# A key projection moved in front of a query projection: the memory attention of a two-block transformer

## The chip, the cores and the metric

The kernel runs on one core of a Trainium2 chip. The metric is the device time of one launch in microseconds, taken as the median over several executions. The clock of TensorE is given as the share that the throttle granted: 1.00 is 2.4 GHz and 0.50 is 1.2 GHz, its two levels.

## What is computed

Two transformer blocks of two layers each run one after the other on 256 tokens of width 1024. The change touches the second block. Cut to what matters, each of its layers computes

```python
x = x + rmsnorm(merged @ w_out[l], norm_mix_post[l])
h = rmsnorm(x, norm_mem_pre[l])
mem_n = rmsnorm(mem, norm_memkv[l])
# memory_cross_attention(h, mem_n, ...), 4 heads of 128
q = (h @ w_q).reshape(b, s, MEM_HEADS, MEM_HEAD_DIM)
kv = mem_n @ w_kv
k, v = kv[..., :MEM_WIDTH], kv[..., MEM_WIDTH:]
sc = jnp.einsum("bshd,bmhd->bhsm", q, k) * (MEM_HEAD_DIM ** -0.5)
o = softmax(sc) @ v
x = x + rmsnorm(o @ w_o, norm_mem_post[l])
```

The keys and values come from the memory input alone. The query needs x after the mixing output's norm. All of it is in float32: each product of two matrices is made of three products of rounded halves (high x low, low x high, high x high).

## The kernel before, in words

**Weights.** All weights of a layer are a stream of chunks of 128 x 1536 floats in the order in which the jobs use them. `Stream.add` packs each job's tiles behind the one before. SP copies chunk c into `raw[c % 5]` as soon as the chunk five before it is free. ScalarE rounds it into a high part (`split_hi`, L639), VectorE subtracts for the low part (`split_lo`, L650). For the chunks in the set `of_pool` GpSimd makes the low part (`pool_lo`, L663); in the second block these were chunks 0 and 1. High and low parts have four buffers each (`SPLIT = 4`), so the high part of chunk c waits until chunk c - 4 is free (`split_free`). That signal is given by the first suitable matmul behind the last one that reads the chunk (`free_split`).

**Jobs.** A job is a projection into one bank: 16 tiles of 128 x 128 (8 for mk0a and mk0b) with three matmuls of 256 columns each. The jobs here and the chunks that hold their weights are

| job | what | chunks before | chunks after the change |
|---|---|---|---|
| out3 | last quarter of the mixing output | 47, 48 | 47, 48 |
| mk0a | key head 0 | 48 | 48 |
| mk0b | key head 1 | 49 | 49 |
| mq0 | query heads 0 and 1 | 49, 50 | 51, 52 |
| mk1 | key heads 2 and 3 | 51, 52 | 49, 50 |
| mq1 | query heads 2 and 3 | 52, 53 | 52, 53 |
| mv | values | 53 to 56 | 53 to 56 |

Most jobs go through `products`, which calls `free_split` on the first of the three matmuls of every tile. mq0 is in `first_products`: it makes all 32 products with the high part of x first, in the order of x's rows, and the 16 products with the low part of x behind them. Only the latter call `free_split`:

```python
ins = nc.tensor.matmul(dst, whi[c % SPLIT][0:rows, o:o + width], lo[0:rows, k, :], start=False, stop=(k == KD - 1),
                       skip_group_check=True)
left[c] -= 1
if (n, t, k) == (name, len(pl.jobs[name].tiles) - 1, KD - 1):
    ins.then_inc(*s.mark("filled", name))
else:
    free_split(pl, ins)
```

**Order.** A list, `order_b`, is written out by hand. Every engine walks it and does its part of each step. Around the change it is: the jobs out0 to out3, mk0a, the norm of the mixing output (`norm` and `spread` of p1), mk0b, then the four `front` steps and `squares` of n2, then mq0, `adds` of n2, mk1, `mean` of n2, the first scores, mq1 and so on. In the steps

- `spread p1`, VectorE scales y and adds it to x (`vector_post`, L2424 and L2426);
- `front n2`, ScalarE writes the high part of x with the gains (`x_hi`, L926) and VectorE the low part (`x_lo`, L958), eight rows of tiles each;
- `squares n2`, ScalarE squares x (L952) and then splits high parts up to mq0's last chunk + 2;
- `job`, ScalarE and VectorE split up to the job's last chunk + 2 (mk0a and mk0b, in `own_splits`, split nothing) and ScalarE evacuates the job's bank;
- `mem_keys`, ScalarE evacuates mk0a or mk0b (L2321);
- `adds n2`, GpSimd adds the first half of the squares (`pool_norm`, L870 and L872) and VectorE the rest (`vector_adds`, L889, L891 and L894);
- `mean n2`, TensorE sums over the partitions (`tensor_mean`, L966), ScalarE takes the root and VectorE the reciprocal. The query isn't scaled by it: the scores are, in the exponential.

mk0a and mk0b were already placed around the norm of the mixing output, to give TensorE work while x is not yet there.

Of the kernel before, what the change touches and what calls it, by code (L numbers as in the profile page):

```python
# [225 lines left out]
def second_jobs(stream):  # L226
# [36 lines left out]
    for i in range(4):  # L263
        job(f"out{i}", "w_out_2", "merged", cols(i * T, 2), full)
    for name, source, operand, i in (("mk0a", "w_mkv_2", "mem", 0), ("mk0b", "w_mkv_2", "mem", 1), ("mq0", "w_mq_2", "x2", 0), ("mk1", "w_mkv_2", "mem", 2),
                                   ("mq1", "w_mq_2", "x2", 2)):
        job(name, source, operand, cols(i * P, 1 if name.startswith("mk0") else 2), full)
# [135 lines left out]
def transformer(nc, known, stream_a, jobs_a, stream_b, jobs_b, const_at,  # L403
                x_in, mem_in, pos_in, w_a, w_b, gains_a, gains_b, consts, out):
    ctx = ExitStack()
    with ctx:
# [1403 lines left out]
        for i in range(4):  # L1810
# [3 lines left out]
        order_b += [("job", "out0"), ("mem_split", 0), ("job", "out1"), ("mem_split", 1), ("job", "out2"), ("root_table", "out"),  # L1814
                    ("job", "out3"), ("job", "mk0a"), ("mem_keys", "mk0a"), ("norm", "p1"), ("spread", "p1"), ("job", "mk0b")]
        order_b += [("front", ("n2", i)) for i in range(4)] + [("squares", "n2"), ("mem_keys", "mk0b"), ("job", "mq0"), ("adds", "n2"), ("job", "mk1"), ("mean", "n2"),
                    ("exp_table", 0), ("mem_scores", 0), ("mem_scores", 1), ("mem_weights", 0), ("mem_weights", 1), ("job", "mq1"),
# [17 lines left out]
        PRE = {"n1": "norm_mix_pre_2", "n2": "norm_mem_pre_2", "n3": "norm_ffn_pre_2"}  # L1835
        own_splits = {"mk0a", "mk0b"} | {f"{u}{i}" for i in range(1, KF2 // 2) for u in ("ua", "ub")} - {"ua1"}
        QK_B = [j for i in range(3) for j in (f"q{i}", f"k{i}")]
# [32 lines left out]
        for kind, name in order_b:  # L1870
# [14 lines left out]
            "h": (HH2, HL2, lambda k: ("hidden_lo", k))}, ("ua", "ub", "ma", "mb", "mc"))  # L1885
        plan_b.of_pool = {0, 1}

# [393 lines left out]
        def scalar_b(act, l):  # L2281
# [4 lines left out]
            for kind, name in order_b:  # L2286
# [31 lines left out]
                elif kind == "mem_keys":  # L2318
                    act.wait_ge(*s.at(l, "filled", name))
                    h = "ab".index(name[-1])  # L2320
                    nc.scalar.activation(MK[:, h, :], pl.bank(name)[:, 0:T], ACT.Copy).then_inc(*s.mark("mem_qk", name))  # L2321
                elif kind == "exp_table":
# [7 lines left out]
                elif kind == "job":  # L2330
# [36 lines left out]
                    elif name.startswith("gate"):  # L2367
                        i = int(name[4:])
                        act.wait_ge(*s.at(l, "gate_in", i))
                        nc.scalar.activation(GT[:, 2 * i:2 * i + 2, :], GT[:, 2 * i:2 * i + 2, :], ACT.Tanh, scale=0.5).then_inc(*s.mark("gate", i))  # L2370

                    elif name.startswith("out") or name.startswith("mo") or name.startswith("down"):
                        scalar_y(pl, act, l, name)
                    elif name in ("mk0a", "mk0b"):
                        continue
                    elif name == "mv":
                        act.wait_ge(*s.at(l, "filled", name))
                        nc.scalar.activation(MVB[:, 0, 0:PAIR], ps[:, :], ACT.Copy).then_inc(*s.mark("values_first", name))
                    elif name.startswith("mk") or name.startswith("mq"):
                        i = int(name[2])  # L2380
                        act.wait_ge(*s.at(l, "filled", name))
                        dst, sc = (MK, 1.0) if name[1] == "k" else (MQ, MEM_D ** -0.5)
                        nc.scalar.activation(dst[:, 2 * i:2 * i + 2, :], two(ps[:, :]), ACT.Copy, scale=sc).then_inc(*s.mark("mem_qk", name))
                elif kind == "chunks":
# [410 lines left out]
```

## Time and profile before

| | |
|---|---|
| runs | 1670.61, 1670.56 and 1667.18 us, median 1670.56 |
| the profiled execution | 1670.88 us, its span 1669.1 us |
| TensorE busy | 1629.8 us (98% of the span) |
| VectorE busy | 1209.8 us (72%) |
| ScalarE busy | 899.5 us (54%) |
| GpSimd busy | 116.3 us (7%) |
| granted clock, mean | 0.994 |

Matmuls overlap in the records: one is shown with 0.28 us and the next starts about 0.12 us behind it. So a busy TensorE is one whose matmuls follow each other without a hole; how fast they follow is seen from their start times. The stretch around the change is at 929 to 949 us in the first layer of the second block and at 1411 to 1430 us in its second layer. In the trace's names PE is TensorE, DVE is VectorE, ACT is ScalarE, POOL is GpSimd.

### The profile page before, as it was taken

The page shows a single profiled execution, that of the slowest core. Times are in us where ns is not written, and L with a number is a line of the kernel's source. Part 1 is how long each engine was busy: PE and PEld are TensorE (multiplying, and loading weights), DVE is VectorE, ACT ScalarE, POOL GpSimd, SP SyncE. Part 2 cuts the span into 40 slices and gives each one's busy share as a digit, 9 for nine tenths or more (in the row PEclk, how much of TensorE's full clock was granted, in tenths as well). Part 3 has the DMA queues.
Part 4 walks back from the last instruction along what each step waited for, and adds up shares of the span by engine and source line. Part 5 has one row for each costly group of instructions (what it writes and reads, how often), then busy time and mean ns, then how long its engine had stood idle before and what let it go on. Part 6 is the DMA issues. An engine that isn't in the chain of part 4 may idle for free.

```text
span 1669.1 us, 31856 instructions
## 1 busy us (share of the span) xinstructions
PE 1629.8 (98%) x13566; PEld 1578.4 (95%) x13566; DVE 1209.8 (72%) x1785; ACT 899.5 (54%) x1378; POOL 116.3 (7%) x72
## 2 busy tenths in 40 slices
PE   9988999999999999999999999999999999999997
PEld 9977999999879999999999989999999999899997
DVE  5887777647976776487858768984777767679963
ACT  5585644454775444544544665554545546655542
POOL 2020000020110000210000110001100001010000
PEclk9999999999999999999999999999999999999999
DMA  8313556553225655565345535655464454446560
GB/s 294 107 65 106 198 191 200 179 193 129 95 60 190 217 190 188 193 213 198 112 152 176 167 118 173 217 174 176 149 221 163 141 161 166 152 137 205 184 208 33
DMA packets 53598, 275.03 MB, mean 165 GB/s; under 512 B 6480, under 2 KB 7376, under 8 KB 53328
## 3 DMA queue, kind: packets, MB, share of 16 engines
q1 hardware_dynamic: 53312, 271.94, 48.1%
q8 instruction: 107, 1.75, 0.4%
q10 hardware_dynamic: 144, 1.05, 0.2%
q14 instruction: 35, 0.29, 0.1%
HBM read 271.13 MB, written 1.05 MB: 163 GB/s over the span
## 4 chain that ended last, share of the span: by engine, by line
PE 81%; DVE 13%; ACT 3%; issue 2%; DMA 0%; SPq 0%; ACTq 0%; DVEq 0%
PE bank L809 17%; PE bank L811 17%; PE bank L812 17%; PE scores L809 3%; PE scores L811 3%; PE scores L812 3%; DVE weights_lo L650 3%; DVE x_lo L958 2%; PE heads L809 2%; PE heads L811 2%; PE heads L812 2%; ACT probs L1229 1%; PE heads L1967 1%; PE scores L818 1%; DVE x L2426 1%
## 5 line engine op out<-in xcount | busy, mean ns | idle before, releaser
L650 DVE TENSOR_TENSOR weights_lo<-raw,weights_hi 128x1536 fp32r<-128x1536 f32 (+2 forms) x344 | 583.0, 1712 | 221.6 <-ACT weights_hi L639 220.9
L639 ACT ACTIVATE weights_hi<-raw 128x1536 fp32r<-128x1536 f32 (+5 forms) x352 | 500.2, 1440 | 173.0 <-PE bank L812 74.5
L809 PE MATMUL bank<-x_hi,weights_lo 128*128 128x256 f32 (+1 forms) x1556 | 433.8, 279 | 0.3 <-DVE weights_lo L650 0.3
L811 PE MATMUL bank<-x_lo,weights_hi 128*128 128x256 f32 (+1 forms) x1556 | 430.9, 277 | 0.0
L812 PE MATMUL bank<-x_hi,weights_hi 128*128 128x256 f32 (+1 forms) x1556 | 430.8, 277 | 0.0
L809 PEld LDWEIGHTS bank<-x_hi,weights_lo 128*128 128x128 f32 (+1 forms) x1556 | 290.6, 187 | 3.5 <-issue 2.7
L811 PEld LDWEIGHTS bank<-x_lo,weights_hi 128*128 128x128 f32 (+1 forms) x1556 | 290.8, 187 | 0.1
L812 PEld LDWEIGHTS bank<-x_hi,weights_hi 128*128 128x128 f32 (+1 forms) x1556 | 290.8, 187 | 0.0
L809 PE MATMUL bank<-hidden_hi,weights_lo 128*128 128x256 f32 x692 | 191.5, 277 | 2.0 <-DVE hidden_lo L2278 2.0
L811 PE MATMUL bank<-hidden_lo,weights_hi 128*128 128x256 f32 x692 | 191.0, 276 | 0.0
L812 PE MATMUL bank<-hidden_hi,weights_hi 128*128 128x256 f32 x692 | 191.0, 276 | 0.0
L809 PEld LDWEIGHTS bank<-hidden_hi,weights_lo 128*128 128x128 f32 x692 | 129.9, 188 | 2.6 <-DVE hidden_lo L2278 2.4
L811 PEld LDWEIGHTS bank<-hidden_lo,weights_hi 128*128 128x128 f32 x692 | 129.9, 188 | 0.0
L812 PEld LDWEIGHTS bank<-hidden_hi,weights_hi 128*128 128x128 f32 x692 | 129.9, 188 | 0.0
L870 POOL TENSOR_TENSOR squares<-squares 128x512 f32<-128x512 f32 x28 | 48.9, 1745 | 969.6 <-ACT squares L2207 799.3
L809 PE MATMUL scores<-x_hi,weights_lo 128*128 128x256 f32 x400 | 110.4, 276 | 0.0
L811 PE MATMUL scores<-x_lo,weights_hi 128*128 128x256 f32 x400 | 110.4, 276 | 0.0
L812 PE MATMUL scores<-x_hi,weights_hi 128*128 128x256 f32 x400 | 110.4, 276 | 0.0
L809 PEld LDWEIGHTS scores<-x_hi,weights_lo 128*128 128x128 f32 x400 | 75.1, 188 | 0.0
L811 PEld LDWEIGHTS scores<-x_lo,weights_hi 128*128 128x128 f32 x400 | 75.1, 188 | 0.0
L812 PEld LDWEIGHTS scores<-x_hi,weights_hi 128*128 128x128 f32 x400 | 75.1, 188 | 0.0
L809 PE MATMUL heads<-x_hi,weights_lo 128*128 128x256 f32 x256 | 71.1, 278 | 0.4 <-DVE weights_lo L650 0.4
(427 smaller groups left out, 3487.3 us busy)
## 6 DMA issues: line engine op xcount, KB each, us to landing
raw<-in_w_b SPq DMA_DIRECT2D x202, 768.0 KB, 4.3
raw<-in_w_a SPq DMA_DIRECT2D x120, 768.0 KB, 4.3
raw<-in_w_a SPq DMA_DIRECT2D x16, 512.0 KB, 3.6
raw<-in_w_a SPq DMA_DIRECT2D x2, 736.0 KB, 8.4
raw<-in_w_a SPq DMA_DIRECT2D x2, 672.0 KB, 6.9
x<-in_x SPq DMA_DIRECT2D x2, 512.0 KB, 5.2
mem<-in_mem ACTq DMA_DIRECT2D x1, 1024.0 KB, 8.3
raw<-in_w_b SPq DMA_DIRECT2D x2, 512.0 KB, 5.4
```

Source lines behind the costliest of these rows:

```text
L639: nc.scalar.activation(whi[c % SPLIT][:, 0:n], raw[c % RAW][:, 0:n], ACT.Copy).then_inc(*s.mark("weights_hi", c))
L650: nc.vector.tensor_tensor(wlo[c % SPLIT][:, 0:n], raw[c % RAW][:, 0:n], whi[c % SPLIT][:, 0:n].bitcast(F32), ALU.subtract).then_inc(*s.mar ...
L809: ins = nc.tensor.matmul(dst, wl, xh, start=start, stop=False, skip_group_check=skip)
L811: nc.tensor.matmul(dst, wh, xl, start=False, stop=False, skip_group_check=skip)
L812: ins = nc.tensor.matmul(dst, wh, xh, start=False, stop=stop, skip_group_check=skip)
L818: ins = nc.tensor.matmul(dst, xl, wh, start=first, stop=False, skip_group_check=True)
L870: nc.gpsimd.tensor_tensor(sq[:, 0:2, :], sq[:, 0:2, :], sq[:, 2 * n:2 * n + 2, :], ALU.add).then_inc(*s.mark("sq_pairs", (tag, n)))
L958: nc.vector.scalar_tensor_tensor(out=XL[:, k, :], in0=X[:, k, :], scalar=gains(k), in1=XH[:, k, :].bitcast(F32), op0=ALU.mult, op1=ALU.sub ...
L1229: ins = nc.scalar.activation(PA[c][:, m, :], score_bank[c][:, m * T:(m + 1) * T], ACT.Exp, scale=f[:, m:m + 1], bias=ROW[:, r + m:r + m + ...
L1967: ins = nc.tensor.matmul(out_bank[rows, m * P:(m + 1) * P], VB[:, kt, f * DHD:(f + 1) * DHD], PTB[:, g * kts + kt, :], start=(n == 0), sto ...
L2426: nc.vector.tensor_tensor(x, x, y, ALU.add).then_inc(*s.mark("x_new", (tag, last)))
```

## The change

The job mk1 is packed and run in front of mq0, directly behind mk0b. Its evacuation becomes a `mem_keys` step behind the squares, and it is put into `own_splits`, so that it splits nothing ahead. The low part of the chunk behind mk1's last (51) goes to GpSimd.

```diff
-    for name, source, operand, i in (("mk0a", "w_mkv_2", "mem", 0), ("mk0b", "w_mkv_2", "mem", 1), ("mq0", "w_mq_2", "x2", 0), ("mk1", "w_mkv_2", "mem", 2),
+    for name, source, operand, i in (("mk0a", "w_mkv_2", "mem", 0), ("mk0b", "w_mkv_2", "mem", 1), ("mk1", "w_mkv_2", "mem", 2), ("mq0", "w_mq_2", "x2", 0),
                                    ("mq1", "w_mq_2", "x2", 2)):
...
-                    ("job", "out3"), ("job", "mk0a"), ("mem_keys", "mk0a"), ("norm", "p1"), ("spread", "p1"), ("job", "mk0b")]
-        order_b += [("front", ("n2", i)) for i in range(4)] + [("squares", "n2"), ("mem_keys", "mk0b"), ("job", "mq0"), ("adds", "n2"), ("job", "mk1"), ("mean", "n2"),
+                    ("job", "out3"), ("job", "mk0a"), ("mem_keys", "mk0a"), ("norm", "p1"), ("spread", "p1"), ("job", "mk0b"), ("job", "mk1")]
+        order_b += [("front", ("n2", i)) for i in range(4)] + [("squares", "n2"), ("mem_keys", "mk0b"), ("mem_keys", "mk1"), ("job", "mq0"), ("adds", "n2"), ("mean", "n2"),
...
-        own_splits = {"mk0a", "mk0b"} | {f"{u}{i}" for i in range(1, KF2 // 2) for u in ("ua", "ub")} - {"ua1"}
+        own_splits = {"mk0a", "mk0b", "mk1"} | {f"{u}{i}" for i in range(1, KF2 // 2) for u in ("ua", "ub")} - {"ua1"}
...
-        plan_b.of_pool = {0, 1}
+        plan_b.of_pool = {0, 1, plan_b.last_chunk("mk1") + 1}
...
                 elif kind == "mem_keys":
                     act.wait_ge(*s.at(l, "filled", name))
-                    h = "ab".index(name[-1])
-                    nc.scalar.activation(MK[:, h, :], pl.bank(name)[:, 0:T], ACT.Copy).then_inc(*s.mark("mem_qk", name))
+                    if name == "mk1":
+                        nc.scalar.activation(MK[:, 2:4, :], two(pl.bank(name)[:, :]), ACT.Copy).then_inc(*s.mark("mem_qk", name))
+                    else:
+                        h = "ab".index(name[-1])
+                        nc.scalar.activation(MK[:, h, :], pl.bank(name)[:, 0:T], ACT.Copy).then_inc(*s.mark("mem_qk", name))
```

ScalarE's order behind the fronts of n2, first as it was. In these listings a tile's number is that of its place in memory, not the chunk's: `weights_hi_57<-raw_50` is chunk 51, `weights_hi_54<-raw_51` is 52, `weights_hi_55<-raw_52` is 53 and `weights_hi_56<-raw_53` is 54.

```order
L952 ACTIVATE squares<-x 128x512 x4
L639 ACTIVATE weights_hi_57<-raw_50 128x1536 [waits split_free,arrived1]
L639 ACTIVATE weights_hi_54<-raw_51 128x1536 [waits split_free,arrived2]
L2321 ACTIVATE mem_k<-bank 128x256 [waits filled]
L2383 ACTIVATE mem_q<-bank 128x512 [waits filled]
L639 ACTIVATE weights_hi_55<-raw_52 128x1536 [waits split_free,arrived3]
L639 ACTIVATE weights_hi_56<-raw_53 128x1536 [waits split_free,arrived4]
L2383 ACTIVATE mem_k<-bank 128x512 [waits filled]
L972 ACTIVATE norm_root<-turned,row 128x4 [waits norm_mean]
```

The same place with the change.

```order
L952 ACTIVATE squares<-x 128x512 x4
L639 ACTIVATE weights_hi_57<-raw_50 128x1536 [waits split_free,arrived1]
L639 ACTIVATE weights_hi_54<-raw_51 128x1536 [waits split_free,arrived2]
L639 ACTIVATE weights_hi_55<-raw_52 128x1536 [waits split_free,arrived3]
L639 ACTIVATE weights_hi_56<-raw_53 128x1536 [waits split_free,arrived4]
L2324 ACTIVATE mem_k<-bank 128x256 [waits filled]
L2321 ACTIVATE mem_k<-bank 128x512 [waits filled]
L2385 ACTIVATE mem_q<-bank 128x512 [waits filled]
L972 ACTIVATE norm_root<-turned,row 128x4 [waits norm_mean]
```

The high parts of 53 and 54 moved in front of the evacuations of mk0b, mk1 and mq0; those of 51 and 52 stayed where they were.

VectorE's order at the same place, first as it was, from the low parts of x to the reciprocal for the mean. The low parts are those of chunks 51, 52, 53 and 54.

```order
L958 SCALAR_TENSOR_TENSOR x_lo<-x,gains_b,x_hi 128x256 [waits norm_hi] x8
L650 TENSOR_TENSOR weights_lo_61<-raw_50,weights_hi_57 128x1536 [waits weights_hi]
L650 TENSOR_TENSOR weights_lo_58<-raw_51,weights_hi_54 128x1536 [waits weights_hi]
L889 TENSOR_TENSOR squares<-squares 128x512 [waits norm_sq]
L891 TENSOR_TENSOR squares<-squares 128x256 [waits sq_last_pairs]
L894 TENSOR_TENSOR squares<-squares 128x256 [waits sq_first,sq_last]
L650 TENSOR_TENSOR weights_lo_59<-raw_52,weights_hi_55 128x1536 [waits weights_hi]
L650 TENSOR_TENSOR weights_lo_60<-raw_53,weights_hi_56 128x1536 [waits weights_hi]
L977 RECIPROCAL token_factor<-norm_root 128x4 [waits norm_root]
```

The same place with the change.

```order
L958 SCALAR_TENSOR_TENSOR x_lo<-x,gains_b,x_hi 128x256 [waits norm_hi] x8
L650 TENSOR_TENSOR weights_lo_58<-raw_51,weights_hi_54 128x1536 [waits weights_hi]
L650 TENSOR_TENSOR weights_lo_59<-raw_52,weights_hi_55 128x1536 [waits weights_hi]
L650 TENSOR_TENSOR weights_lo_60<-raw_53,weights_hi_56 128x1536 [waits weights_hi]
L889 TENSOR_TENSOR squares<-squares 128x512 [waits norm_sq]
L891 TENSOR_TENSOR squares<-squares 128x256 [waits sq_last_pairs]
L894 TENSOR_TENSOR squares<-squares 128x256 [waits sq_first,sq_last]
L977 RECIPROCAL token_factor<-norm_root 128x4 [waits norm_root]
```

The low part of 51 is gone, and the three sums for n2 moved behind the low parts of 53 and 54.

GpSimd's order with the change, from the sums of p1 to those of n2.

```order
L870 TENSOR_TENSOR squares<-squares 128x512 [waits y_sq]
L870 TENSOR_TENSOR squares<-squares 128x512 [waits sq_pairs,y_sq]
L872 TENSOR_TENSOR squares<-squares 128x256 [waits sq_pairs]
L663 TENSOR_TENSOR weights_lo_61<-raw_50,weights_hi_57 128x1536 [waits weights_hi]
L870 TENSOR_TENSOR squares<-squares 128x512 [waits norm_sq]
L872 TENSOR_TENSOR squares<-squares 128x256 [waits sq_pairs]
```

The fourth row, the low part of 51, is new; the others stood in this order before.

## Rows read from the trace of the kernel before

**Rows 1.** The page: busy time (share of the span), and the chain that ended last.

```profile
PE 1629.8 (98%) x13566; PEld 1578.4 (95%) x13566; DVE 1209.8 (72%) x1785; ACT 899.5 (54%) x1378; POOL 116.3 (7%) x72
...
PE 81%; DVE 13%; ACT 3%; issue 2%; DMA 0%; SPq 0%; ACTq 0%; DVEq 0%
```

**Rows 2.** TensorE's waits, 900 to 980 us: waited for, us in total, times, longest.

```profile
PE bank L762 <- DVE x_lo L958: 1.5, 2, 1.0
```

**Rows 3.** mq0's start to mk1's end, both layers: length, busy us (instructions) by engine, PEclk, DMA.

```profile
932.20:948.60 16.40, 14.47 (x98) 13.14 (x98) 15.80 (x20) 11.17 (x16) 2.17 (x2) 0.90 0.35 110
1414.00:1430.00 16.00, 14.22 (x99) 13.04 (x98) 15.86 (x20) 11.18 (x16) 2.17 (x2) 0.89 0.34 104
```

**Rows 4.** TensorE's timeline, first layer: start, duration, instruction; mk0b, mq0, mk1, mk1, mean.

```profile
929.36 0.36 PE L809 MATMUL bank<-mem_hi,weights_lo 128*128 128x256 f32 x1
...
932.27 0.28 PE L751 MATMUL bank<-x_hi,weights_lo 128*128 128x256 f32 x1
...
941.76 0.55 PE L809 MATMUL bank<-mem_hi,weights_lo 128*128 128x256 f32 x1 [0.15 <-DVE weights_lo L650]
...
947.10 0.28 PE L812 MATMUL bank<-mem_hi,weights_hi 128*128 128x256 f32 x1
...
948.63 0.50 PE L966 MATMUL turned<-const,squares 128*128 128x2 f32 x4
```

**Rows 5.** The chain of waits in order of time, 939 to 942 us.

```profile
939.95 1.68 DVE weights_lo L650
941.63 0.14 issue
941.76 0.55 PE bank L809
```

**Rows 6.** Stretches behind and with idle time, columns as in rows 3.

```profile
941.80:944.30 2.50, 2.50 (x12) 2.50 (x13) 2.46 (x3) 2.50 (x3) 0.00 (x0) 0.51 0.65 179
...
141.50:144.70 3.20, 0.38 (x5) 0.04 (x1) 3.10 (x6) 0.00 (x0) 0.00 (x0) 1.00 0.01 3
144.70:148.80 4.10, 4.10 (x23) 4.10 (x24) 3.46 (x7) 1.70 (x7) 0.00 (x0) 0.60 0.67 177
1186.30:1189.50 3.20, 2.59 (x24) 2.39 (x22) 3.20 (x4) 2.31 (x3) 2.95 (x3) 1.00 0.00 0
```

**Rows 7.** ScalarE's timeline, first layer.

```profile
935.32 0.91 ACT L926 ACTIVATE x_hi<-x,gains_b 128x256 fp32r<-128x256 f32 x2 [0.41 <-DVE x L2426]
...
938.22 2.85 ACT L639 ACTIVATE weights_hi<-raw 128x1536 fp32r<-128x1536 f32 x2
...
941.64 0.60 ACT L2383 ACTIVATE mem_q<-bank 128x512 f32<-128x512 f32 x1 [0.32 <-PE bank L762]
```

**Rows 8.** VectorE's timeline, first layer.

```profile
935.20 4.74 DVE L958 SCALAR_TENSOR_TENSOR x_lo<-x,gains_b,x_hi 128x256 fp32r<-128x256 f32 x8
...
943.21 0.68 DVE L889 TENSOR_TENSOR squares<-squares 128x512 f32<-128x512 f32 x1
...
944.38 0.42 DVE L894 TENSOR_TENSOR squares<-squares 128x256 f32<-128x256 f32 x1
```

**Rows 9.** Groups by shape (busy us, mean ns); single POOL sums; one DVE line's range.

```profile
L663 POOL TENSOR_TENSOR weights_lo<-raw,weights_hi 128x1536 fp32r<-128x1536 f32 x4 | 14.0, 3510 | 175.1 <-ACT weights_hi L639 175.1
...
L650 DVE TENSOR_TENSOR weights_lo<-raw,weights_hi 128x1536 fp32r<-128x1536 f32 x318 | 556.1, 1763 | 217.5 <-ACT weights_hi L639 216.8
...
917.22 2.62 POOL L870 TENSOR_TENSOR squares<-squares 128x512 f32<-128x512 f32 x1 [185.19 <-ACT squares L2207]
...
937.41 1.38 POOL L870 TENSOR_TENSOR squares<-squares 128x512 f32<-128x512 f32 x1 [12.47 <-ACT squares L952]
...
L2077 DVE SCALAR_TENSOR_TENSOR mem_lo<-mem,gains_b,mem_hi x16: 473/480/1524, 912.7 to 1402.1; 128x256 fp32r<-128x256 f32 x16
```

**Rows 10.** DMA issues: median us from issue to landing.

```profile
raw<-in_w_b SPq DMA_DIRECT2D x202, 768.0 KB, 4.3
```

**Rows 11.** Second layer: ScalarE's high parts of 51 and 52, TensorE's mean.

```profile
1420.13 2.84 ACT L639 ACTIVATE weights_hi<-raw 128x1536 fp32r<-128x1536 f32 x2
...
1430.08 0.50 PE L966 MATMUL turned<-const,squares 128*128 128x2 f32 x4
```

More of the change, by code:

```diff
@@ L2373, in scalar_b @@
                         scalar_y(pl, act, l, name)
-                    elif name in ("mk0a", "mk0b"):
+                    elif name in ("mk0a", "mk0b", "mk1"):
                         continue
@@ L2381, in scalar_b @@
                         act.wait_ge(*s.at(l, "filled", name))
-                        dst, sc = (MK, 1.0) if name[1] == "k" else (MQ, MEM_D ** -0.5)
-                        nc.scalar.activation(dst[:, 2 * i:2 * i + 2, :], two(ps[:, :]), ACT.Copy, scale=sc).then_inc(*s.mark("mem_qk", name))
+                        nc.scalar.activation(MQ[:, 2 * i:2 * i + 2, :], two(ps[:, :]), ACT.Copy, scale=MEM_D ** -0.5).then_inc(*s.mark("mem_qk", name))
                 elif kind == "chunks":
```

## The prediction, made before the changed kernel ran

> **What bounds the kernel now.** The page comes first: TensorE is busy for 1629.8 of 1669.1 us, and 81% of the chain that ended last is its own, with 13% VectorE's [rows 1]. So a change helps or harms only where TensorE waits, or runs at the lower of its two clock levels. The table of waits around the memory attention (900 to 980 us) names one stall that this change can touch: `x_lo` from VectorE [rows 2]. The stretches from the start of mq0 to the end of mk1 give its full price: 16.4 us in the first layer and 16.0 in the second, for 96 matmuls [rows 3]. At the full clock a matmul of these jobs follows the one before by 0.117 us (13 steps from 947.10 to 948.63 [rows 4]), so 96 need 11.2 us. About 5 us a layer are lost.
>
> The matmul timeline shows how [rows 4]. mk0b's 24 matmuls start at 929.36 and mq0 follows at 932.27. Its products with `x_lo` are held up twice, by 1.0 us at most [rows 2]. mk1 then starts at 941.76, and the chain there does not run through `x_lo` alone: it goes from `x_lo` to the low part of a chunk (939.95 to 941.63) and from there to mk1's first matmul [rows 5]. That is chunk 51, the first that was not split ahead of the norm. Behind the idle time the granted clock is 0.51 for 2.5 us in which 12 matmuls start, one per 0.21 us [rows 6]. The product for the mean starts at 948.63, and I use it as the finishing line of each layer: behind it both programs have the same order.
>
> **What the change does to it, on TensorE first.** The sum is of where that finishing line moves. mk0b and mk1 need chunks 49 and 50, which are split before the norm, and the mem operand, which is complete long before. So mk1 runs at once: 932.27 + 48 x 0.117 = 937.9. By then all of `x_hi` is written (the eight copies end at 936.2 [rows 7]) and `x_lo` nearly (939.9 [rows 8]). The waits on x are gone. This is the announced gain, and if mq0 could run at 937.9 it would be had in full.
>
> It can't. mq0 now sits in chunks 51 and 52, and ScalarE's place for the high part of chunk 51 has not moved: behind the eight `x_hi` and the four squares, at 938.22 [rows 7]. Two high parts take 2.85 us there, so the first is ready at 939.7. Its low part is now GpSimd's. The four 128x1536 subtractions it did elsewhere took 3.51 us each, against 1.76 for one on VectorE [rows 9]. 939.7 + 3.5 = 943.2, and with the 0.14 us from low part to matmul [rows 5] mq0 starts at 943.35. TensorE has then idled 5.4 us in one piece. `x_lo` is complete, so mq0 runs through: 32 products with `x_hi` are 3.75 us. VectorE has the low part of chunk 52 by 941.1 + 1.75 = 942.9 or, if GpSimd holds it off, by 945.0. The first matmul that needs it is the 19th of mq0, no earlier than 945.4. Cost: nothing.
>
> **The clock.** After a stretch of 3.2 us with hardly a matmul (141.5 to 144.7) the granted clock over the following 4.1 us is 0.60, and after this stage's broken idle time it is 0.51. A stretch of 3.2 us with 24 matmuls in it (1186.3) keeps 1.00 [rows 6]. The idle time of 5.4 us is nearest the first. A clock of 0.60 over 4.1 us loses 0.40 x 4.1 = 1.6 us of matmuls. I take 1.6 us for this idle piece. The Trainium skill (TensorE: Matmul & The Clock Gate, section on HAM oscillation) says that long enough idle time throttles the array again, and that the penalty is half of the throttled time. With that rule every idle piece below costs such an amount; were it not to hold here, the sum would be 6.4 us smaller. The 33rd matmul of mq0, the first with `x_lo`, is then at 943.35 + 3.75 + 1.6 = 948.7.
>
> **A second wait that the diff hardly shows.** ScalarE splits ahead to the chunk two behind mq0's last. That was 52 and is 54 now. The buffers of high and low parts are four, so chunk 54 needs the place of 50, and this is given free only by mk1's successor. mq0 is written by `first_products`, which calls `free_split` on its products with `x_lo` and not on those with `x_hi`. So the high part of 54 starts behind 948.7. Queued behind it on ScalarE are the evacuations of mk0b, mk1 and mq0. On VectorE the low part of 54 is ahead of the three sums for n2, which the mean waits for; before, the sums were in front of the low parts of 53 and 54 [rows 8]. The run from matmul to mean: 0.4 (matmul and signal), 1.5 (high), 1.8 (low), 1.6 (three sums, 943.21 to 944.80 [rows 8]), 0.1: 5.4 us. mq0's own last matmul is 1.9 behind the 33rd, so TensorE idles 3.5 us more, with a second low stretch behind it, 1.6 us. GpSimd's two sums for n2 now stand behind its low part. They end by 945.5, or near 949 if VectorE gets in between, and the sum is wanted at 952. Nothing. Root, table load and exponentials stand behind the mean as before, beside mq1. The three evacuations (0.4, 0.6 and 0.6 us, as mq0's [rows 7]) follow the high part of 54 and end by 952.3, before the scores want them. SP's transfers of chunks 56 and 59 wait for the low parts of 51 and 54 and so start some 1.6 and 4 us later. A chunk lands in 4.3 us [rows 10], so 56 is there at 947.6, and mv, the first job that needs it, is behind mq1. I cost them at nothing. The other copies and evacuations are the same ones in another order.
>
> **The sum.** First layer: the mean at 948.7 + 5.4 = 954.1 in place of 948.63 gives +5.5, and the low stretch behind it +1.6: +7.1. Second layer, from its own rows [rows 11]: high part of 51 from 1420.13 to 1421.6, low to 1425.1, mq0 at 1425.25, 33rd matmul at 1430.6, mean at 1436.0 against 1430.08: +5.9, and +1.6. Together +14.6. No later stage gives it back: what follows is a chain led by TensorE with the same waits. The profiled execution took 1670.88 us (span 1669.1), 0.3 above the median of 1670.56, so I forecast 1685.5 in the profile's terms and 1685.2 against the median.
>
> **Bounds of what isn't shown.** Clock: from nothing in all four pieces (-6.4) to twice the loss behind the long idle (+3.2). GpSimd's part at this place: its 3.51 us were measured where VectorE did nothing. Where VectorE subtracts beside it, a 128x512 sum took 2.62 in place of 1.38 [rows 9], so a VectorE subtraction that gets in first adds up to 1.76 a layer. Below 3.5 nothing speaks for. I take 3.5, since chunk 52's high part comes 1.4 us after chunk 51's, and GpSimd is well under way by then.
>
> **The rivals.** *A, the filler does its work* (faster). The 5 us a layer come back: 1670.6 - 5.1 - 4.8 = 1660.7. The point that decides is whether the low part of 51 is there at 937.9. For it speaks that every operand of mk1 is early and that `x_lo` stalls vanish. Against it stands the order: the high part is behind the squares at 938.2, so even an instant GpSimd leaves TensorE idle to 939.8. 3%. *B, one wait only*: the place of chunk 50 is freed in time or the second chain hides beside mq0. Then the mean is at 943.35 + 5.6 + 1.6 = 950.55, +1.9, and +2.4 in the second layer: 1674.9. 6%. *C, GpSimd is held up by VectorE*: as the forecast with up to 1.76 us more a layer, 1688.7. The Trainium skill (SBUF — State Buffer, on the two separate sides) has the port pair of the two engines as an exclusive lock for a whole instruction. The rows agree in kind: one `mem_lo` took 1.52 us in place of 0.48 with GpSimd at work [rows 9]. In this kernel it costs TensorE something if an `x_lo` or chunk 52 slips in front of chunk 51. 10%. *D, no change*: the new waits happen to equal the old 5 us a layer, 1670.6. 2%. *Forecast*: both waits, with one to two low stretches a layer, 79%.
>
> **How the numbers follow.** A measurement here tells 0.2% (3.3 us) from nothing. Only A gives faster: 0.03, and 0.04 with what I have not thought of. D and a lucky B give the same: 0.02. The rest is slower: 0.94. The range takes in the forecast without any clock loss (1678.8), goes halfway from there to B (1676.5), and up past C to 1690 for more clock loss on top. It leaves out A, D and most of B, 11 in 100, and some of the tails.
>
> **What would show it.** Right: a matmul gap of 5 to 6 us after mk1 near 938 and 1420, released by GpSimd's low part; no wait for `x_lo`; a second gap of 3 to 4 us before the product for the mean, released by VectorE's sums, with the low part of 54 just before them; granted clock under 1 behind both. Wrong on the first step: GpSimd's 128x1536 starts before 938. Wrong on the second: the high part of 54 starts before the products with `x_lo`.

## The result, and the profile after

The changed kernel takes 1687.78 us (median of 4 runs, 1685.58 to 1689.75), the kernel before, run beside it, 1669.08 us (median of 4, 1667.18 to 1670.61). The ratio is 1.0111, with a 95% interval of 1.0098 to 1.0124: slower by 18.7 us. The forecast was 1685.2 us with a range of 1676.5 to 1690, and 94 in 100 for slower. The profiled execution took 1689.03 us (span 1687.2).

The page first, busy time and the chain that ended last, against [rows 1]:

```profile
PE 1633.1 (97%) x13566; PEld 1582.5 (94%) x13566; DVE 1210.5 (72%) x1783; ACT 899.3 (53%) x1378; POOL 128.5 (8%) x74
...
PE 81%; DVE 12%; ACT 3%; issue 2%; POOL 0%; DMA 0%; ACTq 0%; DVEq 0%
```

TensorE has the same number of instructions. It is busy 3.3 us longer, and the span is 18.1 us longer, so most of the difference is time in which TensorE waits. GpSimd has two more instructions and 12.2 us more: two low parts of 3.44 us (6.9), and four sums that together take 5.5 us longer, as shown below. The page's shares say no more than that. The waits of TensorE around the memory attention do, with the columns of [rows 2]:

```profile
PE bank L751 <- issue: 5.5, 1, 5.5
PE turned L966 <- DVE squares L894: 3.3, 1, 3.3
```

The wait for `x_lo` is gone, and two others stand in its place. TensorE's timeline places them; the second of these lines answers to [rows 4] (what was mk1's wait there is mq0's here), and the last three are of the second layer:

```profile
939.93 0.28 PE L812 MATMUL bank<-mem_hi,weights_hi 128*128 128x256 f32 x1
945.73 0.55 PE L751 MATMUL bank<-x_hi,weights_lo 128*128 128x256 f32 x1 [5.53 <-issue]
...
951.10 1.98 PE L762 MATMUL bank<-x_lo,weights_hi 128*128 128x256 f32 x16
956.33 1.02 PE L966 MATMUL turned<-const,squares 128*128 128x2 f32 x4 [3.25 <-DVE squares L894]
...
1434.79 0.55 PE L751 MATMUL bank<-x_hi,weights_lo 128*128 128x256 f32 x1 [5.52 <-issue]
...
1441.31 1.98 PE L762 MATMUL bank<-x_lo,weights_hi 128*128 128x256 f32 x16
1446.54 0.61 PE L966 MATMUL turned<-const,squares 128*128 128x2 f32 x4 [3.25 <-DVE squares L894]
```

The first wait is put down to "issue", that is to nothing that the trace shows. GpSimd's line suggests whom it waits for, and the first experiment below confirms it: the low part of chunk 51 ends at 942.19 + 3.44 = 945.63, and mq0 starts 0.10 us later.

```profile
942.19 3.44 POOL L663 TENSOR_TENSOR weights_lo<-raw,weights_hi 128x1536 fp32r<-128x1536 f32 x1 [14.83 <-ACT weights_hi L639]
945.59 2.79 POOL L870 TENSOR_TENSOR squares<-squares 128x512 f32<-128x512 f32 x1
948.46 2.13 POOL L872 TENSOR_TENSOR squares<-squares 128x256 f32<-128x256 f32 x1
```

The second wait is spelled out by the chain of waits in order of time, from mq0's first product with `x_lo` to the mean: the high part of chunk 54, its low part, and three sums.

```profile
951.26 0.13 PE bank L762
951.43 0.04 issue
951.47 1.50 ACT weights_hi L639
953.00 1.76 DVE weights_lo L650
954.75 0.61 DVE squares L889
955.37 0.02 issue
955.39 0.43 DVE squares L891
955.85 0.43 DVE squares L894
```

VectorE's line in the same stretch, against [rows 8], has two more things to read:

```profile
937.63 3.25 DVE L958 SCALAR_TENSOR_TENSOR x_lo<-x,gains_b,x_hi 128x256 fp32r<-128x256 f32 x8
943.52 6.48 DVE L650 TENSOR_TENSOR weights_lo<-raw,weights_hi 128x1536 fp32r<-128x1536 f32 x2 [2.64 <-ACT weights_hi L639]
953.00 1.76 DVE L650 TENSOR_TENSOR weights_lo<-raw,weights_hi 128x1536 fp32r<-128x1536 f32 x1 [3.00 <-ACT weights_hi L639]
```

The eight `x_lo` take 3.25 us where they took 4.74: GpSimd's sums no longer run beside them. The low parts of chunks 52 and 53 take 6.48 us together where two take 3.4: GpSimd's work runs beside these now.

To compare the kernels I use one ruler throughout: the time from mk0b's first matmul of a layer to the first matmul of mq0, its first product with `x_lo`, the mean, mq1's first matmul, and the first matmul of mv, the values' job behind mq1. Both programs have the same order behind mq1. In us, first layer / second layer:

| | mq0 | x_lo | mean | mq1 | mv |
|---|---|---|---|---|---|
| before | 2.91 / 2.82 | 7.54 / 7.55 | 19.27 / 18.81 | 21.25 / 20.79 | 29.41 / 29.15 |
| changed | 13.95 / 13.93 | 19.32 / 20.45 | 24.55 / 25.68 | 28.62 / 28.80 | 37.97 / 37.59 |
| growth | | | +5.28 / +6.87 | +7.37 / +8.01 | +8.56 / +8.44 |

At mq1's start the change has cost 7.37 + 8.01 = 15.4 us, but TensorE's clock is still low there (the rows follow below), and at mv it has cost 8.56 + 8.44 = 17.0 us. The medians are 18.7 us apart, so 1.7 us of the result are not attributed.

The two profiled executions differ by 18.15. They also differ outside the stage: mk0b's first matmul stands at 931.78 in place of 929.36, 2.4 us later, ahead of the change. A stretch near 41 us, in code that is the same in both, ran at the lower clock in this execution. The columns are those of [rows 3], first the changed kernel, then the one before:

```profile
41.00:45.00 4.00, 4.00 (x22) 4.00 (x21) 0.66 (x4) 1.58 (x2) 0.00 (x0) 0.54 0.41 166
```

```profile
41.00:45.00 4.00, 4.00 (x36) 4.00 (x36) 2.04 (x4) 1.59 (x2) 0.00 (x0) 1.00 0.28 112
```

This does not go with the order of jobs. Of the runs below, both with the old order show it too (0.50 and 0.57 in this stretch), and four with the new order have 1.00 there.

The clock in the stage itself (columns as in [rows 3]; in turn the first wait, the 32 products with `x_hi`, and from the mean on, then the last two again in the second layer; the lines of 3.00 us are mq1's start):

```profile
940.00:945.70 5.70, 0.20 (x2) 0.01 (x2) 3.06 (x4) 4.86 (x5) 3.51 (x2) 0.71 0.00 0
945.70:951.10 5.40, 5.37 (x32) 5.40 (x33) 4.30 (x2) 0.00 (x0) 4.81 (x2) 0.67 0.80 251
...
956.30:961.00 4.70, 4.67 (x14) 3.96 (x15) 1.03 (x3) 2.53 (x6) 0.00 (x0) 0.50 0.37 144
960.40:963.40 3.00, 3.00 (x17) 2.91 (x16) 1.75 (x7) 2.50 (x9) 0.00 (x0) 0.59 0.00 0
...
1434.80:1441.30 6.50, 6.50 (x32) 6.50 (x33) 4.26 (x2) 0.00 (x0) 4.77 (x2) 0.54 0.77 247
...
1446.50:1449.70 3.20, 3.16 (x13) 2.64 (x13) 1.03 (x3) 1.97 (x4) 0.00 (x0) 0.67 0.49 202
1449.70:1452.70 3.00, 3.00 (x22) 2.90 (x21) 1.79 (x7) 2.49 (x9) 0.00 (x0) 0.78 0.00 0
```

32 products with `x_hi` take 5.37 and 6.52 us (951.10 - 945.73, 1441.31 - 1434.79) where the full clock needs 3.75. The low clock behind the second wait reaches into mq1. In the kernel before, the same place runs at the full clock:

```profile
950.60:953.60 3.00, 3.00 (x27) 2.97 (x26) 2.17 (x9) 2.99 (x11) 0.00 (x0) 1.00 0.60 223
...
1432.10:1435.10 3.00, 3.00 (x27) 2.97 (x26) 2.18 (x9) 2.99 (x11) 0.00 (x0) 1.00 0.80 258
```

From mq1's first matmul to the next job it was 5.65 and 5.85 us before, and is 6.84 and 6.28 now.

### The profile page after: what moved, and what is told of

It is laid out like the page before. It is cut to its first block, busy times and chain, and to the rows that moved or that the text cites. A ratio compares the mean times of both kernels' runs of the same rounds, so it can differ in the third digit from the quotient of the medians.

```text
span 1687.2 us, 31854 instructions
## 1 busy us (share of the span) xinstructions
PE 1633.1 (97%) x13566; PEld 1582.5 (94%) x13566; DVE 1210.5 (72%) x1783; ACT 899.3 (53%) x1378; POOL 128.5 (8%) x74
## 4 chain that ended last, share of the span: by engine, by line
PE 81%; DVE 12%; ACT 3%; issue 2%; POOL 0%; DMA 0%; ACTq 0%; DVEq 0%
PE bank L809 17%; PE bank L811 16%; PE bank L812 16%; PE scores L809 3%; PE scores L811 3%; PE scores L812 3%; DVE weights_lo L650 3%; PE heads L809 2%; PE heads L811 2%; PE heads L812 2%; DVE x_lo L958 1%; ACT probs L1229 1%; PE bank L751 1%; PE bank L722 1%; PE heads L1967 1%
```

## The experiments

The theory after the result has three terms: chunk 51 is late (its high part stands behind the squares, its low part is on GpSimd), the second wait runs over the place of chunk 50, and each long wait is followed by matmuls at the lower clock. Its rivals: GpSimd's placement is most of the loss; or the waits are shadows of one another, so that removing one gives nothing. Unless it says otherwise, each edit is made to the changed kernel. Eleven kernels ran, in three groups, each beside runs of the kernel before (medians 1670.50, 1670.55 and 1670.26 us).

### The low part of chunk 51 back on VectorE

```
-        plan_b.of_pool = {0, 1, plan_b.last_chunk("mk1") + 1}
+        plan_b.of_pool = {0, 1}
```

> The changed kernel with the low part of chunk 51 back on VectorE, nothing else. Two-wait theory: VectorE is free when the high part is ready and takes 1.75 us in place of GpSimd's 3.4 to 3.5, so the idle time behind mk1 shrinks from 5.5 to 3.8 us in each layer and the second wait stays at 3.3 us: 3.4 us faster than the changed kernel, about 1684. Rival (GpSimd's subtraction is the whole cost, VectorE has the port to itself otherwise): most of the loss of 18.7 us goes, 1675 or less. Rival (the high part on ScalarE is so late that who subtracts does not matter, since VectorE's queue is full): no change, 1687.

Measured: 1683.26 us, ratio 1.0070 (1.0055 to 1.0085). mq0 starts at 12.34 / 12.35 on the ruler, 1.6 us sooner in both layers, and the mean at 22.95 / 21.29. So the engine of this one subtraction is worth 1.6 us a layer directly, and 2.9 and 3.0 at mv (35.09 / 34.58) with what the clock adds. That mq0 moves with this subtraction shows what the first wait is for; the trace calls it "issue" here too, though VectorE does the work. Most of the loss is still there: GpSimd is a part of it, not its cause.

### The three sums ahead of mq0's low parts

```
-        ... ("mem_keys", "mk1"), ("job", "mq0"), ("adds", "n2"), ("mean", "n2"), ...
+        ... ("mem_keys", "mk1"), ("adds", "n2"), ("job", "mq0"), ("mean", "n2"), ...
```

> The changed kernel with VectorE's three sums for n2 in front of the low parts of 52 to 54. Two-wait theory: the mean no longer waits for the low part of 54, but mq0's evacuation on ScalarE is still behind the high part of 54, so the scores wait: idle time before the scores about 1.6 us in place of 3.3 before the mean. But the sums need GpSimd's own sums, which stand behind its low part, so VectorE waits for them until about 947 and delays the low part of 52, which mq0 needs at its 19th matmul, by 2 to 3 us. Net between 3 us faster and 3 us slower than the changed kernel, 1685 to 1691. Rival (there is one wait only and the sums do not matter): no change in any of the two idle times.

Measured: 1677.46 us, ratio 1.0038 (1.0023 to 1.0053), better than I expected. mq0 at 13.92 / 13.93, its `x_lo` products at 19.86 / 20.15, the mean at 21.67 / 21.97, only 1.8 us behind them. I had feared that the low part of chunk 52, now behind sums that wait for GpSimd, would hold up mq0 in the middle. VectorE's and GpSimd's lines show why it did not:

```profile
943.53 1.27 POOL L870 TENSOR_TENSOR squares<-squares 128x512 f32<-128x512 f32 x1
944.88 0.73 POOL L872 TENSOR_TENSOR squares<-squares 128x256 f32<-128x256 f32 x1
```

```profile
945.72 0.43 DVE L894 TENSOR_TENSOR squares<-squares 128x256 f32<-128x256 f32 x1 [5.82 <-POOL squares L872]
946.06 3.42 DVE L650 TENSOR_TENSOR weights_lo<-raw,weights_hi 128x1536 fp32r<-128x1536 f32 x2
```

VectorE does wait 5.82 us for GpSimd, but meanwhile it does nothing beside it, and the two sums take 1.27 and 0.73 us in place of 2.79 and 2.13, and two low parts 3.42 in place of 6.48. What the wait costs, the missing overlap gives back. The second wait is therefore real and separate: without it the kernel takes 10 us less (9.6 on the ruler at mv). A rest stays, as expected, though smaller: TensorE waits 0.9 us in front of the scores for mq0's evacuation, which is still behind the high part of 54.

### The place of chunk 50 given free sooner

`first_products` gives places free with mq0's products with `x_hi` too:

```
-                nc.tensor.matmul(dst, wlo[c % SPLIT][0:rows, o:o + width], hi[0:rows, k, :], start=n not in begun, stop=False, skip_group_check=True)
+                ins = nc.tensor.matmul(dst, wlo[c % SPLIT][0:rows, o:o + width], hi[0:rows, k, :], start=n not in begun, stop=False, skip_group_check=True)
+                if name == "mq0":
+                    free_split(pl, ins)
```

> The changed kernel, with mq0's first product allowed to signal that chunk 50 is free; before, only its products with x_lo did. Two-wait theory: the high part of 54 starts with mq0 in place of 5.4 us later, the sums are done before mq0's end or at most 1 us behind it, and the second idle time of 3.3 us goes with the loss of clock behind it. 4 to 6 us a layer: 1676 to 1680. The first idle time stays 5.5 us. Rival (the mean waits for GpSimd's sums or for VectorE's backlog): the second idle time stays above 2 us and the time above 1684.

Measured: 1676.42 us, ratio 1.0036 (1.0020 to 1.0052), as expected. ScalarE's high part of chunk 54 now follows mq0's first matmul and not its 33rd:

```profile
944.69 1.48 ACT L639 ACTIVATE weights_hi<-raw 128x1536 fp32r<-128x1536 f32 x1 [1.51 <-PE bank L751]
```

mq0 is at 13.93 in both layers, the mean at 22.18 / 21.99; of the second wait 0.9 us are left in the second layer. Two edits that share nothing but the chain of the second wait, each cutting it at another link (here the start of its high part, above the sums behind its low part), give 10 to 11 us in the runs, and 9.6 and 10.3 on the ruler at mv. That shows the chain which the prediction read out of `free_split`.

### Is it the clock? Idle products in the first wait

`WAITS` holds numbers of idle products, products of zeros that nobody reads, which TensorE issues ahead of a job. mq0 gets 45, then 23:

```
-        WAITS = {"p1_sum": 3, "p1_factor": 3, "p2_sum": 7, "p2_factor": 3, "ua0": 7, ...
+        WAITS = {"p1_sum": 3, "p1_factor": 3, "p2_sum": 7, "p2_factor": 3, "mq0": 45, "ua0": 7, ...
```

> The changed kernel with 45 idle products (128 columns of zeros) in front of mq0, which fill the first idle time and change nothing else. Clock theory: the granted clock stays 1.00 through mq0, whose 32 products with x_hi take 3.7 us in place of 5.4 and 6.5, so 1.7 and 2.8 us a layer, 4.5 us in all: 1683. Rival (the slow products are not a matter of the clock but of late chunks): no gain, or 0 to 1 us lost to the dummies.

Measured: 1689.65 us, ratio 1.0113 (1.0095 to 1.0130), no gain. I had the length wrong by a factor of two: one unit of the number shows as two products in the trace. mq0 started at 18.5, 4.6 us later than in the changed kernel, held up by the idle products themselves. But the clock held, and the products with `x_hi` took 3.86 us. So the run was repeated at half the number:

> As e4 but with 23 idle products in front of mq0. In e4 the 45 took 0.22 us each, 9.9 us, and held mq0 up 4.6 us beyond chunk 51; 23 take 5.1 us and end before the low part of 51. Clock theory: mq0 starts 13.9 us behind mk0b's start as in the changed kernel, its products with x_hi take 3.9 us as in e4 in place of 5.4 and 6.5, the rest as before: 4 us faster than the changed kernel, 1684. Rival (they steal nothing but also save nothing): 1688.

Measured: 1681.94 us, ratio 1.0070 (1.0051 to 1.0089). The 46 idle products fill the wait, in TensorE's timeline and in the stretches with it and behind it:

```profile
939.20 5.30 PE L722 MATMUL bank<-quiet 128*128 128x128 f32 x46
```

```profile
938.00:945.50 7.50, 7.47 (x66) 7.28 (x65) 4.86 (x6) 5.71 (x7) 4.46 (x2) 1.00 0.05 7
945.50:949.60 4.10, 4.10 (x38) 4.10 (x38) 3.35 (x2) 0.95 (x1) 3.87 (x2) 1.00 0.87 312
```

mq0 starts where it did (13.88 / 13.90), and its 32 products with `x_hi` take 3.75 us in both layers in place of 5.37 and 6.52. The mean comes 1.7 and 2.8 us sooner with no wait removed: this is the clock's share of the first wait, measured alone. At mv 3.4 of these 4.5 us are left (36.18 / 35.95), since in the second layer the clock costs more behind the second wait than it did without the idle products. The rule of the Trainium skill (TensorE: Matmul & The Clock Gate, on HAM oscillation), that idle time throttles the array and that activity keeps it at its full clock, agrees with these rows.

### GpSimd's part in the old order

The kernel before, with chunk 51's low part on GpSimd and nothing else changed:

```
-        plan_b.of_pool = {0, 1}
+        plan_b.of_pool = {0, 1, 51}
```

> The kernel before, with the order of its jobs unchanged, and only the low part of chunk 51 moved to GpSimd: the change's other half alone. mk1 needs it at 12.4 us behind mk0b's start; GpSimd has it at 13.9. The chain runs through it, so 1.5 us a layer, and GpSimd's sums behind it end at about 18.8, before the mean is wanted at 20.5: 3 to 4 us slower than before, 1674. Rival (GpSimd takes work off VectorE, which is in the chain there): faster than before, 1669 or less. Rival (GpSimd's late sums hold the mean): 1677 or more.

Measured: 1676.45 us, ratio 1.0034 (1.0023 to 1.0045). Slower as expected, but by 5.9 us and not 3 to 4. The mean comes at 21.26 / 21.78, 2.0 and 3.0 us later than before. mk1 now waits 3.5 us for GpSimd in each layer. The rival that GpSimd's late sums hold the mean had 1677 or more, close to the time measured, but the trace excludes it: the last sum ends at 949.56, and the mean starts at 952.32 without a wait. The rows show the toll on both engines:

```profile
941.47 3.44 POOL L663 TENSOR_TENSOR weights_lo<-raw,weights_hi 128x1536 fp32r<-128x1536 f32 x1 [15.46 <-ACT weights_hi L639]
944.86 2.81 POOL L870 TENSOR_TENSOR squares<-squares 128x512 f32<-128x512 f32 x1
```

```profile
942.80 3.73 DVE L650 TENSOR_TENSOR weights_lo<-raw,weights_hi 128x1536 fp32r<-128x1536 f32 x1 [2.64 <-ACT weights_hi L639]
946.45 1.77 DVE L889 TENSOR_TENSOR squares<-squares 128x512 f32<-128x512 f32 x1
```

GpSimd's sum takes 2.81 in place of 1.38, VectorE's low part 3.73 in place of 1.76 and its sum 1.77 in place of 0.68. The part of the change that was to relieve VectorE loads it in fact: its busy time is 1211.1 us with two subtractions fewer, against 1209.8.

### Both waits shortened at once, in two ways

First all three edits so far together: VectorE for chunk 51, places given free sooner, sums ahead of mq0.

> The changed order with both waits shortened as far as the queue allows: low part of 51 on VectorE, chunk 50 freed by mq0's first product, the three sums in front of the low parts. mq0 at 12.3 us behind mk0b's start, 5.6 us of products and 1.5 us of clock, mean at 19.5 against 19.3 and 18.8 before: within 2 us of the kernel before, 1669 to 1673. The theory says that no gain is left as long as the high part of 51 stands behind the squares. Rival (the filler hides the norm once GpSimd is out of the way): 1663 or less.

Measured: 1677.49 us, ratio 1.0041 (1.0026 to 1.0056). A miss, where I had expected 1669 to 1673: no better than the sums ahead (1677.46) or the place given free sooner (1676.42) alone. mq0 is at 13.87 / 13.88 again and not at 12.3. VectorE's line has the reason, my own third edit:

```profile
935.97 4.74 DVE L960 SCALAR_TENSOR_TENSOR x_lo<-x,gains_b,x_hi 128x256 fp32r<-128x256 f32 x8
...
941.81 0.43 DVE L896 TENSOR_TENSOR squares<-squares 128x256 f32<-128x256 f32 x1
942.15 6.76 DVE L650 TENSOR_TENSOR weights_lo<-raw,weights_hi 128x1536 fp32r<-128x1536 f32 x4
```

The sums now stand ahead of the low part of chunk 51 (the first of the four in the last row), on which mq0 waits. With that edit left out, two remain:

> The changed kernel with the low part of chunk 51 on VectorE and the places of mq0's chunks given free by its products with x_hi; the three sums stay behind mq0. This is the joint edit of two runs ago without its reordering of the sums. Theory (the reordering put x_lo and the sums in front of the low part of 51, nothing else spoiled the joint edit): mq0 is back at 12.3 us behind mk0b's first matmul, the products with x_lo start at 17.7 and 16.1 as with VectorE alone, the mean follows 1.8 us behind them (19.5 and 17.9), mq1 another 3 us on, 4.0 and 4.5 us a layer better than VectorE alone: 1674 to 1676. Rival (the early high part of 54 takes ScalarE or the place and so holds mq0): mq0 at 13.9, 1677 or more. Neither has it below the kernel before by more than 0.1%.

Measured: 1672.10 us, ratio 1.0017 (1.0008 to 1.0026). mq0 at 12.35 / 12.37, the `x_lo` products at 17.67 / 17.65, the mean at 19.49 / 19.46, mq1 at 22.00 / 21.97. The miss is explained. The time is 2 us under my forecast, which was counted from the median of the run with VectorE alone; that lies 1.7 us above its own ruler at mv. The mean of the second layer was forecast at 17.9 and comes 1.6 us later, since the products with `x_hi` ran at the lower clock there too. The ruler at mv gives 2.1 us more than before, and 1.8 were measured. TensorE still idles 3.9 us in front of mq0, and 0.4 us in front of the scores for mq0's evacuation. So with both of the change's secondary costs removed, the new order is about level with the old one (1.8 us slower, with an interval of 1.3 to 4.3), and no better, as long as ScalarE makes the high part of chunk 51 behind the squares.

### Chunks 51 and 52 split ahead of the norm's work

Two new steps in the order call the split routines of ScalarE (`hi_to`) and VectorE (`lo_to`) early; chunk 51 is on VectorE.

```
-                    ("job", "out3"), ("job", "mk0a"), ("mem_keys", "mk0a"), ("norm", "p1"), ("spread", "p1"), ("job", "mk0b"), ("job", "mk1")]
+                    ("job", "out3"), ("job", "mk0a"), ("hi_to", 51), ("mem_keys", "mk0a"), ("norm", "p1"), ("hi_to", 52), ("lo_to", 51), ("spread", "p1"), ("lo_to", 52), ("job", "mk0b"), ("job", "mk1")]
...
+                elif kind == "hi_to":
+                    split_hi(pl, act, l, name)
...
+                elif kind == "lo_to":
+                    split_lo(pl, dve, l, name)
```

> The changed kernel with chunks 51 and 52 split ahead of the norm's work, as its only edit besides VectorE for the low part of 51; the second wait is left in (the high part of 54 still behind the products with x_lo). Theory: mq0 at 8.3 us behind mk0b's first matmul, its products with x_lo at 12, and then the chain high of 54, low of 54, three sums: the mean at 17.3 to 17.6 instead of 24.6, mq1 at 20.6: 15.5 us under the changed kernel for both layers, 1669 to 1672, level with the kernel before. Rival (the late chunk 51 is the whole loss, the second wait is only a shadow of it): as the best version, 1664.

Measured: 1672.95 us, ratio 1.0015 (1.0006 to 1.0024). There is no wait in front of mq0 (8.56 / 8.27); the second one is left, 3.6 us in both layers, and the mean is at 17.96 / 17.95. That is 0.4 us later than expected, and mq1 comes at 21.43 / 22.03 and not at 20.6, so the time is 1 us above my range. The rival, that the late chunk is the whole loss (1664), falls.

The next kernel has this edit (with chunk 51 on VectorE), the sums ahead of mq0 as above, and ScalarE's squares of n2 splitting ahead by one chunk in place of two, so that the evacuations of mk0b and mk1 stand ahead of the high part of chunk 54:

```
-                    split_hi(pl, act, l, pl.last_chunk({"n1": "q0", "n2": "mq0", "n3": "ua0"}[name]) + 2)
+                    split_hi(pl, act, l, pl.last_chunk({"n1": "q0", "n2": "mq0", "n3": "ua0"}[name]) + (1 if name == "n2" else 2))
```

> The changed order with chunks 51 and 52 split ahead of the x chain: high part of 51 behind out3's evacuation, high part of 52 behind the root of p1, low part of 51 on VectorE in front of its norm products and of 52 behind them; sums for n2 in front of mq0's splits, and ScalarE's splits behind the squares up to 53 in place of 54. Two-wait theory: mq0 starts at 8.6 us behind mk0b's start, no idle time, no loss of clock, mean at 14.3 to 15 against 19.3 and 18.8 before. 4 to 5 us a layer: 1660 to 1663. Rival (the x chain is delayed by the 1.8 us low part and the stall comes back as a wait for x_hi or x_lo): 1666 or more. Rival (the splits delay the norm of p1 itself, so that mk0b starts later): 1668.

Measured: 1664.10 us (1662.40 to 1664.78), ratio 0.9963 (0.9949 to 0.9978). **It beats both kernels**, by 6.4 us against the one before, though it is 1 us above the 1660 to 1663 that I expected. mq0 at 8.26 / 8.57, the mean at 14.62 / 14.63, mq1 at 16.76 / 16.78, 4.5 and 4.0 us sooner than before. TensorE's only wait there is 0.2 us (for the mean, in both layers), and the clock stays at 1.00 from mk0b to the mean (mk0b and mk1; products with `x_hi`; products with `x_lo`):

```profile
930.80:939.10 8.30, 8.30 (x76) 8.30 (x75) 8.13 (x13) 5.88 (x11) 0.00 (x0) 1.00 0.31 98
939.10:942.70 3.60, 3.60 (x34) 3.60 (x33) 3.60 (x7) 3.56 (x6) 2.29 (x2) 1.00 0.63 221
942.70:945.50 2.80, 2.58 (x19) 2.01 (x17) 2.73 (x7) 1.71 (x2) 0.00 (x0) 1.00 0.01 2
```

Is that the filler's doing or only the early splits'? The kernel before, in its own order of jobs, with the same early splits:

> The kernel before, with its own order of jobs, and nothing but chunks 51 and 52 split ahead of the norm's work. If the early splits are what made the best version fast, mk1 starts without a wait behind mq0, only the stalls for x_lo stay (1.0 us) and the mean comes at 15.3 us behind mk0b's first matmul instead of 19.3 and 18.8: 7.5 us less, 1663 to 1665. If the order with mk1 as filler is what made it, the kernel stays at 1668 or more. In between, 1666, each has half.

Measured: 1676.19 us, ratio 1.0032 (1.0019 to 1.0045). The early splits alone do not make the kernel fast; it is the second of my two cases (1668 or more), and worse than the kernel before by 5.9 us. The rows say why (VectorE, TensorE's waits, and the stretch behind them with the columns of [rows 3]):

```profile
937.73 1.75 DVE L650 TENSOR_TENSOR weights_lo<-raw,weights_hi 128x1536 fp32r<-128x1536 f32 x1
939.39 4.73 DVE L958 SCALAR_TENSOR_TENSOR x_lo<-x,gains_b,x_hi 128x256 fp32r<-128x256 f32 x8
```

```profile
PE bank L762 <- DVE x_lo L958: 1.8, 3, 1.0
PE bank L751 <- ACT x_hi L926: 0.6, 1, 0.6
```

```profile
944.00:948.00 4.00, 4.00 (x19) 3.89 (x20) 1.58 (x4) 1.49 (x2) 0.00 (x0) 0.50 0.01 4
```

Early splits put two low parts ahead of `x_lo` on VectorE, which starts 8.25 us behind mk0b's first matmul and not 5.84. In the old order mq0 needs `x_lo` at that time. It waits, its matmuls and mk1's behind it run at the lower clock, and the mean comes at 22.26 / 20.91. In the new order mk1 covers it. My forecast overlooked this, and also that the old order hardly waited for chunk 51 at all: [rows 4] has that wait at 0.15 us. So the gain of 6.4 us needs three things together: the filler, the early splits, and the second chain cut. With the last left out it is +2.7 us against before, with the early splits left out +1.8, and with the early splits alone, in the old order, +5.9.

## Why the prediction was right

**Direction and size.** Forecast +14.6 us, measured +18.7 in the runs and +17.0 on the ruler at mv. The time lies in the range, 2.6 us above the forecast. The mechanism came as forecast, both waits and the low clock behind each; one kind of term was too small.

**mk1 runs at once, the waits on x are gone.** Right: no wait for `x_lo` in this stage.

**First wait.** Forecast 5.4 us, ended by GpSimd's low part; measured 5.53 and 5.52. The trace names no releaser; the run that gives the subtraction to VectorE, and has mq0 1.6 us sooner, shows that it is the low part. mq0 was forecast 13.99 us behind mk0b's first matmul and came at 13.95 / 13.93. The 3.51 us taken for GpSimd were 3.44 here.

**The clock behind it.** The term of 1.6 us was right in the first layer (5.37 - 3.75 = 1.62) and too small in the second (6.52 - 3.75 = 2.77). The run with 46 idle products returned just these, 1.7 and 2.8.

**Second wait.** Forecast 5.4 us from the 33rd matmul to the mean; measured 5.23 in both layers (956.33 - 951.10), by the very chain that was named. Two runs that break it at different links each gave back 10 to 11 us. The rows give 3.25 us of waiting, the forecast 3.5.

**The clock behind that.** From the mean to mq1 before: 1.98 us; after: 4.07 and 3.12. From mq1 to the job behind it, before: 5.65 and 5.85; after: 6.84 and 6.28. Together that is 3.3 and 1.6 us for the 1.6 forecast. The four clock terms come to 9.2 us in place of 6.4. They are mis-sized by 2.8 us, and the rest of the sum had some 0.4 too much: together the ruler's difference from the forecast (17.0 against 14.6). The forecast took one size, 1.6 us, from one stretch elsewhere. Two of the four came out at it and two at nearly twice that, so the size was in part luck. The bounds that it gave for the clock, up to 3.2 us more, do hold the 2.8.

**What was costed at nothing.** The low part of chunk 52 was not waited for, though GpSimd held it up; the sums on GpSimd ended at 950.59 and were wanted at 955.85; no wait on a transfer appeared. All stood.

**Rivals.** A (filler works, 1660.7) needed mq0 at 937.9, and fell. But its mechanism is sound: with chunks 51 and 52 early and the second chain cut it gave 1664.1. B (one wait, 1674.9) fell, though the runs that remove the second wait, 1676.4 and 1677.5, are close to its price. C (GpSimd held up by VectorE in front of chunk 51) fell: GpSimd got in first. The holding-up runs the other way, and it is clear in the rows: sums of 2.79 and 2.13 where they took 1.38 and 0.79, and a low part on VectorE that starts at 943.52, 1.33 us behind GpSimd's. The exclusive lock of the port pair (Trainium skill, SBUF — State Buffer, on the two separate sides) agrees with each of them. D (no change) fell.

**Open.** The 1.7 us by which the runs differ beyond the ruler. The other kernels' rulers to mv miss their medians by -2.2 to +1.9 us, so it is no more than these scatter. Why the same wait cost the clock 1.6 us in one layer and 2.8 in the other was not tested.

## What to carry to other kernels

Filler moves the bound only if the job that follows it has its operands ready when the filler ends: moving a job back also moves forward what it reads (here a weight chunk whose split stood behind the norm's squares), so move the preparation with it. Look at ring buffers when jobs change places, since the step that frees a place moves too. An order and its preparation are one change: here the order alone cost 18.7 us (1.8 with its side costs removed) and the early splits alone 5.9, while both together, with the place of chunk 50 no longer in the way of the mean, gained 6.4.

## What the runs showed of the hardware

- GpSimd beside a busy VectorE slows both. A 128x512 sum on GpSimd takes 1.27 us with VectorE waiting and 2.79 with it subtracting; eight `x_lo` on VectorE take 3.25 us alone and 4.74 beside two sums on GpSimd; one low part 1.76 or 3.73. Letting VectorE wait for 5.82 us cost little: 1677.5 us, against 1676.4 for the run that cuts the same chain at its other link.
- One wait of 5.5 us is followed by a loss to the clock of 1.6 us in one layer and 2.8 in the other, at the same place in the same program. Behind the wait of 3.6 us that is left with chunk 51 on VectorE (the first experiment), it was 1.6 us in one layer and nothing in the other. Such a term has no single value. It also reaches further than the first matmuls: behind the wait of 3.25 us, mq1 still ran at 0.59 and 0.78 for its first 3 us.
- An idle product of 128x128 takes 0.115 us (46 in 5.30), the same as the working 128x256 ones follow one another at, and keeps the granted clock at 1.00.
- The profile does not always name whom TensorE waits for. mq0's wait for the low part of chunk 51 appears as "issue", whether GpSimd makes it (5.5 us) or VectorE (3.6 us); mk1's wait for it in the old order appears under GpSimd's name (3.5 us).
